# A hybrid GLA and retention decoder step on one core: the opening of block 0 reordered, with 18 spare transposes on TensorE

## What is computed

```python
def _layer(x, s_gla, s_ret, ...):
    h = rmsnorm(x, norm_w)
    z = h @ w_in                  # q,k,v,gate of GLA; 16 low-rank gate columns; q,k,v,gate of retention
    la = log_sigmoid(glr @ gla_w2 + gla_b) / 16        # forget gate of GLA
    q_b, k_b = rope(rq), rope(rk)                      # retention
    o_a, s_gla = gla(q_a, k_a, v_a, la, s_gla)         # chunked for the prompt, one step for the sample
    o_b, s_ret = retention(q_b, k_b, v_b, s_ret)
    mixed = concat(rmsnorm(o_a) * silu(gg), (groupnorm(o_b) * w + b) * silu(rg))
    return x + mixed @ w_out, s_gla, s_ret
# two layers, a final rmsnorm; outputs are both y and the four sets of states
```

## Time and profile before

| what | value |
|---|---|
| median of 3 runs | 1684.18 us (1683.59 to 1684.27) |
| time of the profiled execution | 1683.42 us |
| its span, first to last instruction | 1681.6 us |
| PE busy | 1658.7 us, 99% of the span |
| DVE, ACT, POOL busy | 59%, 37%, 50% |
| mean DMA rate | 148 GB/s |
| mean granted TensorE clock | 0.999 |

### The profile page before, as it was taken

How to read it: one execution, slowest core, us unless ns; L and a number is a source line. 1 busy time by engine, 2 the same in 40 slices (tenths; PEclk the granted TensorE clock), 3 DMA queues, 4 the chain that set the end, 5 groups by cost and what they waited for, 6 DMA issues and landing times.

```text
span 1681.6 us, 26257 instructions
## 1 busy us (share of the span) xinstructions
PE 1658.7 (99%) x9898; PEld 1362.6 (81%) x9898; DVE 994.5 (59%) x2340; ACT 613.8 (37%) x1159; POOL 837.9 (50%) x661
## 2 busy tenths in 40 slices
PE   6999999999999999999999999999999999999998
PEld 4888878888788887888878888788887888878886
DVE  7733575856765375454755346757677464784453
ACT  4423344233342333433343233332334333343332
POOL 4445445554454544555444454556545455454545
PEclk9999999999999999999999999999999999999999
DMA  7534357653564444753546534478444753453624
GB/s 263 164 106 122 101 202 223 186 156 126 182 181 119 120 138 138 163 153 93 157 132 151 134 88 152 166 171 223 130 154 138 163 145 94 143 172 91 163 90 142
DMA packets 311902, 249.54 MB, mean 148 GB/s; under 512 B 218464, under 2 KB 220896, under 8 KB 311776
## 3 DMA queue, kind: packets, MB, share of 16 engines
q1 hardware_dynamic: 237904, 113.36, 25.6%
q10 hardware_dynamic: 73872, 134.51, 24.5%
HBM read 209.12 MB, written 38.67 MB: 147 GB/s over the span
## 4 chain that ended last, share of the span: by engine, by line
PE 96%; DMA 1%; DVE 1%; SPq 0%; issue 0%; ACT 0%; ACTq 0%; POOLq 0%; POOL 0%; DVEq 0%
PE bank L716 82%; PE bank L975 3%; PE bank L981 2%; PE bank L779 1%; PE bank L959 1%; PE bank L937 1%; PE bank L916 1%; PE bank L683 1%; PE bank L1007 1%; PE bank L920 1%; PE bank L737 1%; PE bank L992 0%; PE bank L789 0%; PE bank L895 0%; DMA w_stage<-in_w_slots 0%; DMA out_k_rows<-region 0%
## 5 line engine op out<-in xcount | busy, mean ns | idle before, releaser
L269 POOL TENSOR_TENSOR w_lo<-w_stage,w_hi 128x512 fp32r<-128x512 f32 x264 | 363.1, 1396 | 332.6 <-ACT w_hi L262 332.6
L716 PE MATMUL bank<-h_hi,w_hi 128*128 128x512 f32 x1024 | 408.0, 398 | 3.9 <-DVE h_lo L356 3.9
L716 PE MATMUL bank<-h_lo,w_hi 128*128 128x512 f32 x1024 | 399.8, 390 | 0.0
L716 PE MATMUL bank<-h_hi,w_lo 128*128 128x512 f32 x1024 | 399.4, 390 | 0.0
L269 POOL TENSOR_TENSOR w_lo<-ss,w_hi 128x512 fp32r<-128x512 f32 x164 | 219.3, 1358 | 224.6 <-ACT w_hi L262 224.6
L262 ACT ACTIVATE w_hi<-w_stage 128x512 fp32r<-128x512 f32 x264 | 152.7, 624 | 349.1 <-PE bank L716 315.1
L716 PEld LDWEIGHTS bank<-h_hi,w_hi 128*128 128x128 f32 x1024 | 192.4, 188 | 55.2 <-issue 7.6
L716 PEld LDWEIGHTS bank<-h_hi,w_lo 128*128 128x128 f32 x1024 | 192.5, 188 | 41.2
L716 PEld LDWEIGHTS bank<-h_lo,w_hi 128*128 128x128 f32 x1024 | 192.6, 188 | 37.1
L716 PE MATMUL bank<-w_hi,m_hi 128*128 128x512 f32 x512 | 202.9, 396 | 0.0
L716 PE MATMUL bank<-w_hi,h_hi 128*128 128x512 f32 x512 | 200.7, 392 | 0.0
(11 more groups left out here) (214 smaller groups left out, 2180.4 us busy)
## 6 DMA issues: line engine op xcount, KB each, us to landing
w_stage<-in_w_slots ACTq DMA_DIRECT2D x264, 256.0 KB, 3.2
ss<-in_w_slots ACTq DMA_DIRECT2D x164, 256.0 KB, 3.1
v_b<-in_w_slots ACTq DMA_DIRECT2D x84, 256.0 KB, 3.0
region<-in_x_prompt SPq DMA_DIRECT2D x32, 512.0 KB, 4.4
xn<-in_x_t SPq DMA_DIRECT2D x16, 512.0 KB, 4.8
out_k_rows<-region SPq DMA_DIRECT2D x32, 256.0 KB, 3.8
k_n<-out_k_rows SPq DMA_DIRECT2D x256, 32.0 KB, 2.7
out_o_rows<-region SPq DMA_DIRECT2D x32, 256.0 KB, 2.0
```

The source lines that it names most:

```text
L269: pool.tensor_tensor(w_lo[:, r, c], stage(h), w_hi[:, r, c].bitcast(f32), ALU.subtract).then_inc(lo_done, 1)
L716: i = pe.matmul(P[q][:, :], x, y, start=(s == 0 and kk == 0 and c == 0), stop=(s == 3 and kk == 1 and c == 2), skip_group_check=True)
```

## The change

Four things change, all of them in block 0 of layer 0.

- PE: `scale_rows` issues 8 transposes of the identity into bank X between its first and its second pair, and 10 behind the second pair (`idle_turns`). Nothing reads them.
- ACT: `h_hi` of K tile 0 is rounded before `w_hi` of half 1, and the loads of halves 4 and 5 are issued behind `h_hi` of K tile 1.
- PE, ACT, DVE: `hT_slot0` and the sample's gate go from before slot 2 (and from within it) to behind slot 2; `gate_expand` goes from slot 2 to slot 3 (behind group 1), and all that follows the gate moves one slot down: the small matmuls of the sample's gate from slot 2 to 3, ACT's Abs, Exp, Ln from 2 to 3, `la` from slots 3 and 4 to 4 and 5, `al` from slot 4 to slot 5. `z_transposed` of slot 6 now also waits for `al` (`V_LA`), and the first sample projection of slot 2 for `hs` (`V_H`). In the second layer's first block these two waits are there too.
- DVE: `sample_norm` goes two K tiles forward, the mask `gmask` behind `sample_start`, and `next_stats` of block 1 from slot 2 to slot 8; POOL's root of it from slot 8 to 9.

```diff
--- before.py
+++ after.py
@@ -364,9 +364,18 @@
                 pe.wait_ge(rstd_x.sem, rstd_x.at(m, 1))
             for t in range(TPB):
                 if m == 0 and t % 2 == 0:
+                    if t > 0:
+                        idle_turns(pe, 8)
                     pe.wait_ge(first_rs, t // 2 + 1)
                 i = pe.transpose(ATT[:, TOK * t:TOK * t + TOK], factor[:, t:t + 1].to_broadcast([128, 128]), ident[:, :])
             i.then_inc(ht_ps.sem, KT)
+            if m == 0:
+                idle_turns(pe, 10)
+
+        def idle_turns(pe, count):
+
+            for _ in range(count):
+                pe.transpose(X[:, 0:128], ident[:, :], ident[:, :])
 
         def next_scaled(vec, m, k):
             if k == 0:
@@ -638,7 +647,7 @@
                         if w == 2 and 0 < n <= NBLK:
                             pool.wait_ge(ystat.sem, ystat.at(n - 1, 4))
                             rsqrt(xrs_1[:, n - 1, :], yvar[:, :], rstd_y.sem)
-                        if w == 8 and n < NBLK - 1:
+                        if w == (9 if n == 0 else 8) and n < NBLK - 1:
                             pool.wait_ge(xstat.sem, xstat.at(n + 1, 4))
                             rsqrt(xrs[:, :], xvar[:, :], rstd_x.sem)
                         if w in (15, 20) and kind == 1:
@@ -682,7 +691,7 @@
                                 r = slice(64 * hf + 32 * (k % 2), 64 * hf + 32 * (k % 2) + 32)
                                 i = pe.matmul(ATT[r, 0:256], wg[:, k, :], x_t[:, k, 256 * hf:256 * hf + 256], start=(k < 2), stop=(k >= 6))
                         i.then_inc(slot_used, 1)
-                        if kind == 0 and n > 0:
+                        if kind == 0:
                             sample_gate()
 
                     def sample_gate():
@@ -752,6 +761,7 @@
                         i.then_inc(slot_used, 1)
 
                     def unit_slot(u, s):
+                        w = 4 * u + s + 1
                         first = n * HALVES + 2 * (4 * u + s)
                         pe.wait_ge(lo_done, first + 2)
                         if n == 0 and u == 0:
@@ -762,17 +772,16 @@
                             if u == 6 and s == 2:
                                 pe.wait_ge(mlo_sb.sem, mlo_sb.at(n, 4 + q + 1))
                             i = products(u, s, q)
-                            if n == 0 and u == 0 and s == 1:
-                                if q == 0:
-                                    sample_transposed(0)
-                                if q == 1:
-                                    gate_expand()
-                                if q == 2:
-                                    sample_gate()
+                            if n == 0 and w == 2 and q == 0:
+                                sample_transposed(0)
+                            if n == 0 and w == 3 and q == 1:
+                                gate_expand()
                             if q < 3 and s == 3:
                                 i.then_inc(proj.sem, 1)
                         if kind == 0 and u < 6 and s % 2 == 1:
                             if s == 1:
+                                if u == 0:
+                                    pe.wait_ge(s_v.sem, s_v.at(l, V_H))
                                 free_sample_bank(u)
                             for k in range(2 * s - 2, 2 * s + 2):
                                 for c in range(4):
@@ -831,12 +840,13 @@
 
                     def sample_work(w):
                         if kind == 0:
-                            if w == 2:
+                            if w == 2 + int(n == 0):
                                 pe.wait_ge(lrs_sb.sem, lrs_sb.at(l, 1))
                                 for q in range(2):
                                     i = pe.matmul(X[:, 144 + 8 * q:152 + 8 * q], w2b[0:32, 128 * q:128 * q + 128], lr_s[:, :], start=True, stop=True)
                                 i.then_inc(gx_ps.sem, 1)
                             if w == 6:
+                                pe.wait_ge(s_v.sem, s_v.at(l, V_LA))
                                 z_transposed(X[:, 256:384], 0)
                             if w == 13:
                                 pe.wait_ge(o_sb.sem, o_sb.at(n, 4))
@@ -1013,7 +1023,6 @@
                         u, s = (w - 1) // 4, (w - 1) % 4
                         if n == 0 and w == 1:
                             first_slot()
-                            hT_slot0()
                             continue
                         if n == LAST and w == SLOTS - 2:
                             last_slots()
@@ -1023,6 +1032,8 @@
                         unit_slot(u, s)
                         if w == 1:
                             gate_expand()
+                        if n == 0 and w == 2:
+                            hT_slot0()
                         if kind > 0:
                             g = w // 21
                             if w in (9, 21):
@@ -1070,11 +1081,13 @@
             load_half(act, 2)
             load_half(act, 3)
             split_hi(act, 0)
+            next_hi(act, 0, 0)
             split_hi(act, 1)
-            load_half(act, 4)
-            load_half(act, 5)
-            for k in range(KT):
+            for k in range(1, KT):
                 next_hi(act, 0, k)
+                if k == 1:
+                    load_half(act, 4)
+                    load_half(act, 5)
                 if k in (3, 5):
                     split_hi(act, (k + 1) // 2)
             for l in range(DEPTH):
@@ -1098,10 +1111,10 @@
                             nc.scalar.activation(o_d[:, w // 18, :], (ATT, ST)[w // 18][:, :], ACT.Copy).then_inc(od_sb.sem, 1)
                         if kind != 0:
                             return
-                        if w == 2:
+                        if w == 2 + late:
                             act.wait_ge(lrs_ps.sem, lrs_ps.at(l, 1))
                             nc.scalar.activation(lr_s[0:RANK, :], X[0:RANK, 128:136], ACT.Copy).then_inc(lrs_sb.sem, 1)
-                        if w == 3:
+                        if w == 3 + late:
                             act.wait_ge(gx_ps.sem, gx_ps.at(l, 1))
                             nc.scalar.activation(gt[:, :], X[:, 144:160], ACT.Abs).then_inc(gl_s.sem, 1)
                             act.wait_ge(gl_s.sem, gl_s.at(l, 1))
@@ -1122,10 +1135,11 @@
                                 nc.scalar.activation(sg_s[:, 32 * g:32 * g + 32].rearrange("p (a b) -> p a b", b=8), z_t[:, 4 + 8 * g:8 + 8 * g, :],
                                                      ACT.Tanh, scale=0.5).then_inc(tg_s.sem, 1)
 
+                    late = int(n == 0)
                     for w in range(SLOTS):
 
-                        if w == (1 if n > 0 else 2):
-                            act.wait_ge(slot_used, n * SLOTS + (1 if n > 0 else 2) + RING)
+                        if w == (1 if n > 0 else 3):
+                            act.wait_ge(slot_used, n * SLOTS + w + RING)
                             act.wait_ge(const_in, 96)
                             nc.scalar.activation(lr_t, ATT[:, 0:256], ACT.Identity, bias=bias_row[:, :]).then_inc(lr_sb.sem, 1)
                         if w == 5:
@@ -1275,10 +1289,8 @@
                     sample_stats(0)
                 if k == 3:
                     sample_mean(0)
-                if k == 7:
+                if k == 5:
                     sample_norm(0)
-            vec.wait_ge(const_in, 96)
-            vec.tensor_scalar(gmask[:, :], rmask[:, 0:TOK], 0.0, None, ALU.is_gt)
             for l in range(DEPTH):
                 def body(l, n, kind):
                     def done(k):
@@ -1420,7 +1432,7 @@
 
                     def sample_work(w):
                         if kind == 0:
-                            if w == 4:
+                            if w == 4 + late:
                                 sample_gate()
                             if w == 8:
                                 sample_q_ret()
@@ -1645,13 +1657,16 @@
                             vec.tensor_tensor(buf, buf, r_tmp[:, :], ALU.add).then_inc(rope_st.sem, 1)
                             c += 4
 
+                    late = int(n == 0)
                     if n == 0:
                         sample_start(l)
+                        vec.wait_ge(const_in, 96)
+                        vec.tensor_scalar(gmask[:, :], rmask[:, 0:TOK], 0.0, None, ALU.is_gt)
                     for w in range(1, SLOTS):
                         if kind == 0 and w == 2:
                             clear_states()
-                        if w in (3, 4):
-                            hf = w - 3
+                        if w in (3 + late, 4 + late):
+                            hf = w - 3 - late
                             vec.wait_ge(gate_l.sem, gate_l.at(n, 5 + hf))
                             half_la = la[:, :, 256 * hf:256 * hf + 256]
                             vec.wait_ge(o_ps.sem, o_ps.at(n, 0))
@@ -1728,7 +1743,7 @@
                             sample_state_gla(w - 16)
                         if w == 18:
```

(2 more changed lines are left out.)

## The result

| | before | after |
|---|---|---|
| median of 5 runs each, us | 1684.18 | 1693.00 |
| lowest and highest, us | 1683.26 to 1684.73 | 1691.40 to 1694.27 |
| profiled execution, us (span) | 1683.42 (1681.6) | 1691.96 (1690.2) |
| mean granted TensorE clock | 0.999 | 0.995 |

The ratio is 1.0053, with an interval of 1.0040 to 1.0065: the changed kernel is 8.8 us slower. The forecast was slower, 1691.0 in a range of 1687.2 to 1693.2.

What follows compares the result with a forecast made beforehand. TensorE, without a hole from 24.74 us on, was taken to bound the kernel. Transposes 0, transpose place at slot 6 +6.2 and clock +1.4 gave +7.6 us on 1683.42, so 1691.0 us, range 1687.2 to 1693.2.

Steps and rivals of the forecast that it cites:

- the rival with the chance of 0.04: Both chains, to al and to the first scores, are longer: all steps shared, a second cold stretch; +9 to +11 us.
- The transposes at 0: Start, slot 1: the 18 added transposes fit TensorE's idle time and neither cost nor win anything, 0 us.
- Slot 2 from 24.0, waiting for `w_lo`: TensorE starts slot 2 at 24.0 us instead of 26.67, waiting for GpSimd's w_lo of halves 2 and 3.
- slot 3, forecast for 33.9: TensorE starts slot 3 at 33.9 us against 36.27; of these 2.4 us, 1.6 are only owed.
- `la` set by ScalarE, 41.5: VectorE's la begins at 41.5 us, after ScalarE's first Ln; the 6.7 us of statistics leaving this place bring nothing.
- The wait for `al`, 5.8 us, place +6.2: TensorE waits 5.8 us at slot 6's transpose for al behind rotate, going on at 66.7, 6.2 us later than before.
- The bound of 6 us for all twelve steps alone: VectorE's rotate: if all twelve two-input steps ran unshared, at most 6 us would come off.
- The statistics at slot 8, hidden by the first wait: Statistics before the first scores put these at 86.1 us, asked for at 85.2; 0.9 us, covered by the clock's loss.
- Alone would cost 6.7 us: Statistics at slot 8: without the wait for al, their delay of the first scores would cost 6.7 us.
- The clock, +1.4: Behind the wait for al TensorE's clock falls, costing 1.4 us, with products 0.43 us apart for some 3 us.
- The rival in which the clock stays up (0.3): TensorE's clock stays up through the wait for al: +6.2 to +7.1 us, 1689.6 to 1690.5; chance 0.3.
- Not slower: Rotate is ahead of TensorE, al there by 60.5 us, or statistics don't delay scores: 1681.5 to 1683 us; chance 0.05.

Runs made afterwards that it cites:

- experiment 5: Changed kernel with al back before rotate, statistics of block 1 back at slot 2, and without the 18 transposes: 1684.25 us, ratio 1.0003 to the kernel before.
- experiment 6: Kernel before with only the 18 transposes of the identity added: 1683.85 us, ratio 1.0002.
- experiment 4: Changed kernel without the 18 transposes of the identity: 1691.86 us, ratio 1.0041 to the kernel before.
- experiment 1: Changed kernel with al made before the rotation again: 1692.75 us, ratio 1.0050 to the kernel before.
- experiment 2: Changed kernel with the statistics of block 1 back at slot 2: 1691.70 us, ratio 1.0044 to the kernel before.
- experiment 3: Changed kernel with both repairs, al back before rotate and the statistics of block 1 back at slot 2: 1684.63 us, ratio 1.0003 to the kernel before.
- experiment 10: Kernel before with al alone moved behind the rotation and the transpose at the end of slot 6 waiting for it: 1687.31 us, ratio 1.0020.
- experiment 11: Changed kernel with statistics of block 1 back at slot 2 and gate_expand behind group 0 of slot 3: 1691.83 us, ratio 1.0046 to the kernel before.
- experiment 7: Changed kernel with statistics of block 1 back at slot 2 and 42 unread transposes before the wait for al: 1689.54 us, ratio 1.0034 to the kernel before.

## Why the prediction was right, step by step

It was right in direction, in place and in mechanism, 2.0 us below the median; some of its terms were off in ways that cancelled. The median of 1693.0 lies only 0.2 us inside the range (1687.2 to 1693.2), and two of the five runs above it. By its number it would also fit the rival with the chance of 0.04 (1692.4 to 1694.4), but what that rival names, all steps of the rotation shared and a second cold stretch, wasn't there: it had four long steps of twelve, and one slow stretch behind the wait.

- *The transposes at 0*: right for the kernel before and the one with both repairs (experiments 5 and 6); in the changed kernel experiment 4 leaves up to 1.1 us open. The clock they were to lift they did lift, and in six of eight profiles it fell again, see below.
- *Slot 2 from 24.0, waiting for `w_lo`*: 24.1 to 24.3, with this wait, in the profiles of experiments 1 to 4, but 25.52 and without it in the profile after:

```profile
25.52 0.39 PE L725 MATMUL bank<-h_hi,w_hi 128*128 128x512 f32 x1
...
26.89 0.38 PE L707 MATMUL bank<-ident,o_d 128*128 128x128 f32 x2
```

In this execution the identity's DMA let TensorE begin at 9.39 (8.60 in experiment 4), the first product came at 15.87 (15.07), and `w_lo` ended at 25.04 (24.24). Slot 1, whose products ran 0.43 us apart from 17.56 to 23.2, ended 0.5 behind that. This delay ran on: slot 3, forecast for 33.9, began at 34.61, `la` at 42.75 (41.65 in experiment 4), the outputs at 87.56 (86.56). That the two profiled executions are alike all the same (1691.96 and 1692.10) is by 1.1 us of waits for `k_n` in experiment 4.
- *`la` set by ScalarE, 41.5*: 42.75, behind a slot 3 that was 0.7 late; 41.4 to 41.7 in experiments 1 to 4. That the statistics which leave this place bring nothing was right: VectorE stood idle before `la` for 13.6 us.
- *The wait for `al`, 5.8 us, place +6.2*: 4.75 us and +6.3. TensorE came to it 1.1 us later than forecast (62.1) and `al` at 66.60, forecast 66.7. This hit is partly luck, for two errors cancelled: the rotation began 1.0 us late and took 17.5 us, not 18.4. I took its length as given by GpSimd's equal work; experiments 10 and 11 show 16.5 and 18.4 us by how the two engines' steps meet. The bound of 6 us for all twelve steps alone came from a mean; by its five long steps it is 5. Only the range that I gave this term was sound, not the reason for its value.
- *The statistics at slot 8, hidden by the first wait*: the scores were masked at 87.42 where TensorE asked at 87.5, forecast 86.1 and 86.6. "Alone would cost 6.7 us" was nearly the size of it: the profiled execution of experiment 1 is 6.9 us longer than that of before, 5.4 of it by the place of the first outputs (84.43 against 79.03) and the rest by slow outputs; its median is 8.5 longer.
- *The clock, +1.4*: 12.94 us instead of 10.92, so +2.0. This is the term that was mis-sized. I priced it by the cold start, 3 us of slow products; here they were slow from 66.94 to 71.36, 4.4 us. Nor is 2.0 a fixed price: slots 7 and 8 lost 1.2 us in the profile of experiment 11, 1.6 in 10, 2.1 in 4 and 2.2 in 2. The rival in which the clock stays up (0.3) fell: behind this wait the clock didn't stay up of itself in any of these five profiles, and with the wait filled it did (experiment 7).
- *Not slower*: the sum for its condition is off. For `al` by 60.5, 6.2 us before 66.7, `la` would have to begin at 35.3, 6.2 before 41.5, not at 34.6. It changes nothing; `la` never began before 40.

The sum was +7.6 us against +8.5 in the profiled execution: of the 0.9 between them 0.6 is the clock, 0.1 the place of the transpose and 0.2 the transpose itself, which took 0.48 us instead of 0.26. Where I was least careful was not in the sum: asked what the move of `al` alone does to the kernel before, I said 7 us for experiment 10, and it was 3 (4.8 in the profiled execution). There both the start and the length of the rotation were favourable.

## What to carry to other kernels

Where one engine is busy throughout, write the others' due times beside its calendar, and check every moved step for all that stood behind its old place and now stands ahead of it: a start that is 2 us earlier is worth nothing if a result 40 us on has become 6 us late. Repair suspected waits one at a time and together, since two waits in a row hide each other, and a repair that brings nothing alone may be half of what is needed. A chain of short VectorE steps beside GpSimd's work had no fixed length here (16.5 to 18.4 us); price it as a range.

## What the runs showed of the hardware

**The clock fell behind a shorter hole than I thought, and not at once.** In the profile of experiment 10 the hole before the transpose is 2.8 us. TensorE after it (start us, us, engine, line):

```profile
64.61 0.41 PE L716 MATMUL bank<-w_lo,h_hi 128*128 128x512 f32 x1
64.84 0.61 PE L716 MATMUL bank<-w_hi,h_lo 128*128 128x512 f32 x1
65.25 0.63 PE L716 MATMUL bank<-w_hi,h_hi 128*128 128x512 f32 x1
```

The products start 0.23 us apart until 64.84, 1.3 us after work resumed, and then 0.43 until 68.24; slots 7 and 8 took 12.55 us, 1.6 more than in the earlier trace rows.

**Transposes lifted the clock, and in most executions it fell again behind short waits.** TensorE at its start, kernel after:

```profile
15.87 0.47 PE L725 MATMUL bank<-h_hi,w_hi 128*128 128x512 f32 x1 [1.67 <-DVE h_lo L356]
16.17 0.39 PE L725 MATMUL bank<-h_lo,w_hi 128*128 128x512 f32 x1
...
17.56 0.77 PE L725 MATMUL bank<-h_hi,w_hi 128*128 128x512 f32 x1 [0.76 <-DVE h_lo L356]
18.12 0.63 PE L725 MATMUL bank<-h_lo,w_hi 128*128 128x512 f32 x1
```

The first three products start 0.30 and 0.23 us apart, at the fast level, where those of the kernel before were slow. All eight profiles with the 18 transposes begin like this, and all five without them begin slow. Then, behind waits of 1.67 and 0.76 us, the rest of slot 1 is slow until 23.2. In experiments 3 and 6 the same happened from 16.8 to 19.9 and from 17.5 to 20.6; in the profiles of experiments 1 and 2, with waits of 1.2 or 1.3 and 0.76 us, the products in a row stayed 0.22 to 0.24 us apart. Why one execution keeps it and the other doesn't stays open.

**A two-input step of VectorE that stands beside a `w_lo` of GpSimd can take 1.62 to 1.82 us instead of 0.69.** In the thirteen profiles each long step of the rotation has 1.1 us or more of a `w_lo` beside it. Not every meeting does this: steps with up to 0.55 us of a `w_lo` beside them kept their 0.69, and a few that lay wholly inside a pair took 0.74 to 0.99. The mean of 1.2 in the earlier trace rows was a mixture of short and long steps.
